# The second mixer's post norm, residual and first feed-forward units, worked in two token sets

## The reference, cut to what matters

```python
def rms_norm(x, g):
    xf = x.astype(jnp.float32)
    y = xf * lax.rsqrt(jnp.mean(xf * xf, axis=-1, keepdims=True) + EPS)
    return (y * g.astype(jnp.float32)).astype(x.dtype)

mix = jnp.matmul(y, w_out)                        # 1024 x 1024: "wo2"
x = x + rms_norm(mix, norm_mix_post)              # "post"
hn = rms_norm(x, norm_ffn_pre)                    # "ffn2"
g = dwconv3(jnp.matmul(hn, w_gate), conv_w, conv_b)
u = jnp.matmul(hn, w_up)                          # 1024 x 2816 each
ff = jnp.matmul(jax.nn.gelu(g, approximate=True) * u, w_down)
x = x + rms_norm(ff, norm_ffn_post)
```

## Time and profile before

| | |
|---|---|
| time, median of 3 runs | 1293.77 us (1291.98 to 1294.85) |
| the profiled execution's own time | 1292.15 us |
| its span in the trace | 1290.3 us |
| PE, PEld busy | 1273.3 us (99%), 1041.1 us (81%) |
| DVE, ACT, POOL busy | 690.6, 394.1, 756.7 us |
| HBM read | 114.71 MB, 91 GB/s over the span |
| granted TensorE clock, mean | 0.997 of full speed |

### The profile page before, as it was taken

How to read it: one execution, slowest core, us unless ns; L and a number is a source line. 1 busy time by engine, 2 the same in 40 slices (tenths; PEclk the granted TensorE clock), 3 DMA queues, 4 the chain that set the end, 5 groups by cost and what they waited for, 6 DMA issues and landing times.

```text
span 1290.3 us, 16120 instructions
## 1 busy us (share of the span) xinstructions
PE 1273.3 (99%) x6432; PEld 1041.1 (81%) x6432; DVE 690.6 (54%) x924; ACT 394.1 (31%) x717; POOL 756.7 (59%) x448
## 2 busy tenths in 40 slices
PE   8999999999999999999999999999899999999998
PEld 6888877888888888888887878778788888888886
DVE  5453563867544432123467878685687744447003
ACT  4332474322111111003246365573322211110002
POOL 5854533676666646768665445224659766666660
PEclk9999999999999999999999999999899999999999
DMA  7222211323333323333233122102133333333231
GB/s 287 82 68 81 82 50 50 111 88 95 98 98 99 99 72 114 90 100 122 96 110 94 55 82 81 35 18 82 50 131 98 98 96 93 95 96 96 97 98 66
DMA packets 34207, 117.85 MB, mean 91 GB/s; under 512 B 3812, under 2 KB 4324, under 8 KB 34004
## 3 DMA queue, kind: packets, MB, share of 16 engines
q1 hardware_dynamic: 32976, 114.66, 28.3%
q10 hardware_dynamic: 1156, 2.16, 0.5%
HBM read 114.71 MB, written 2.10 MB: 91 GB/s over the span
## 4 chain that ended last, share of the span: by engine, by line
PE 97%; DVE 1%; DMA 1%; ACT 1%; issue 0%; POOL 0%; SPq 0%; DVEq 0%; ACTq 0%
PE PS L466 29%; PE PS L468 28%; PE PS L467 28%; PE PS L1083 2%; PE PS L968 1%; PE PS L692 1%; PE PS L669 1%; PE PS L500 1%; PE PS L559 1%; PE PS L501 1%; PE PS L680 1%; PE PS L503 1%; PE PS L951 1%; DMA RAW<-in_w 1%; PE PS L1064 0%; PE PS L942 0%
## 5 line engine op out<-in xcount | busy, mean ns | idle before, releaser
L423 POOL TENSOR_TENSOR WL<-RAW,WH 128x1024 fp32r<-128x1024 f32 (+1 forms) x216 | 509.9, 2361 | 18.0
L420 POOL TENSOR_SCALAR WH<-RAW 128x1024 fp32r<-128x1024 f32 (+1 forms) x216 | 234.2, 1084 | 442.8 <-DMA RAW<-in_w 399.8
L466 PE MATMUL PS<-AH,WH 128*128 128x512 f32 x896 | 351.3, 392 | 2.8 <-DVE AL L1759 1.5
L468 PE MATMUL PS<-AH,WL 128*128 128x512 f32 x896 | 348.8, 389 | 0.0
L467 PE MATMUL PS<-AL,WH 128*128 128x512 f32 x896 | 348.7, 389 | 0.0
L466 PEld LDWEIGHTS PS<-AH,WH 128*128 128x128 f32 x896 | 168.2, 188 | 41.6 <-POOL WL L423 2.4
L468 PEld LDWEIGHTS PS<-AH,WL 128*128 128x128 f32 x896 | 168.2, 188 | 35.2
L467 PEld LDWEIGHTS PS<-AL,WH 128*128 128x128 f32 x896 | 168.3, 188 | 34.5 <-issue 0.2
L1409 ACT ACTIVATE TMP<-PAD,PRM 128x512 f32<-128x512 f32 x44 | 35.9, 816 | 122.5 <-DVE PAD L2022 122.5
L466 PE MATMUL PS<-SH,WH 128*128 128x512 f32 x176 | 68.5, 389 | 0.0
L467 PE MATMUL PS<-SL,WH 128*128 128x512 f32 x176 | 68.5, 389 | 0.0
(11 more groups left out here) (365 smaller groups left out, 2036.0 us busy)
## 6 DMA issues: line engine op xcount, KB each, us to landing
RAW<-in_w SPq DMA_DIRECT2D x185, 512.0 KB, 3.5
RAW<-in_w SPq DMA_DIRECT2D x16, 384.0 KB, 3.1
RAW<-in_w SPq DMA_DIRECT2D x16, 320.0 KB, 2.8
X<-in_x SPq DMA_DIRECT2D x4, 512.0 KB, 7.4
BT<-in_bias SPq DMA_DIRECT2D x1, 2048.0 KB, 9.5
out<-FX SPq DMA_DIRECT2D x4, 256.0 KB, 2.1
out<-FX ACTq DMA_DIRECT2D x4, 256.0 KB, 2.0
PIN<-in_p ACTq DMA_DIRECT2D x1, 512.0 KB, 3.4
```

Of the source, the lines that this page charges most:

```text
L420: nc.gpsimd.tensor_scalar(WH[:, slot, 0:width], RAW[:, slot, 0:width], 1.0, 1.0, ALU.mult, ALU.mult).then_inc(s_hi, 1)
L423: nc.gpsimd.tensor_tensor(WL[:, slot, 0:width], RAW[:, slot, 0:width], WH[:, slot, 0:width].bitcast(F32), ALU.subtract).then_inc(s_split, 1)
L466: nc.tensor.matmul(o, lh, rh, start=start, stop=False)
L468: return nc.tensor.matmul(o, ll, rh, start=False, stop=stop)
```

## The change

The last two projection units and the first four feed-forward units are computed in two token sets, tokens 0 to 255 and 256 to 511 (`HALVES`), each as 256-column matmuls, and so are all steps between them.

- Projection: units 4 and 5 stay whole and go to banks 4 and 5 (no wait any more for a bank to be copied). Units 6 and 7 run for the first set into banks 2 and 3, then for the second set into banks 4 and 5, which wait for `s_mix`.
- Post norm: `post_sum` on VectorE adds the two last squares of a set, `post_columns` takes two columns from `ACC` alone, `post_reciprocal` and `post_diagonal` make one diagonal each on VectorE and ScalarE, `post_broadcast` spreads them into bank 7 (first set) or bank 6 (second). On TensorE those of the first set stand inside the projection's second set, those of the second set inside the feed-forward's first set, at k = 4 and k = 6.
- Residual and pre norm: VectorE takes the 8 tiles of the first set (`post_added`, `post_low`), then their 8 squares in a row (`post_squared`), then the same for the second set. `statistic` waits for all 16 and stands ahead of the last k of the second set.
- POOL splits weights up to the fourth feed-forward unit, then waits until all 16 low parts are made, and splits the fifth and sixth after that. Before it had no wait there.

```diff
-            split_range(UNITS["wo2"][0] + 4, UNITS["ffn2"][0] + NS)
-            split_range(UNITS["ffn2"][0] + NS, NU)
+            split_range(UNITS["wo2"][0] + 4, UNITS["ffn2"][0] + 4)
+            ge(pool, s_gl["ffn2"], 2 * DK)
+            split_range(UNITS["ffn2"][0] + 4, NU)
...
-            def side_by_side(u0, banks, hi, lo, each, before):
-                for n in range(len(banks)):
+            def post_halves(u0, hi, lo, high, low, between):
+                for n in range(4):
...
-                        for n, b in enumerate(banks):
+                for half, c in enumerate(HALVES):
+                    for k in range(DK):
+                        if (half, k) in between:
+                            between[half, k]()
+                        ge(pe, high, DK * half + k + 1)
+                        for n in range(4):
                             s = (u0 + n) % NS
-                            if part == 0:
-                                nc.tensor.matmul(pb[b], WH[:, s, tokens(k)], hi[:, k, :], start=(k == 0), stop=False)
-                                nc.tensor.matmul(pb[b], WL[:, s, tokens(k)], hi[:, k, :], start=False, stop=False)
-                            else:
-                                ins = nc.tensor.matmul(pb[b], WH[:, s, tokens(k)], lo[:, k, :], start=False,
-                                                       stop=(k == DK - 1))
-                                if k == DK - 1:
-                                    ins.then_inc(s_used, 1)
+                            nc.tensor.matmul(pb[n][:, c], WH[:, s, tokens(k)], hi[:, k, c], start=(k == 0), stop=False)
+                            nc.tensor.matmul(pb[n][:, c], WL[:, s, tokens(k)], hi[:, k, c], start=False, stop=False)
+                        ge(pe, low, DK * half + k + 1)
+                        for n in range(4):
+                            s = (u0 + n) % NS
+                            ins = nc.tensor.matmul(pb[n][:, c], WH[:, s, tokens(k)], lo[:, k, c], start=False,
+                                                   stop=(k == DK - 1))
+                            if half and k == DK - 1:
+                                ins.then_inc(s_used, 1)
...
-                ge(pe, s_acc[n], DK)
+                ge(pe, s_acc[n], 2 * DK if n == "ffn2" else DK)
...
-            def root_columns(n):
-                ge(pe, s_acc[n], DK - 1)
-                for part, src in enumerate((ACC, SQ[:, 1, :])):
-                    if part:
-                        ge(pe, s_sq[n], DK)
-                    for t in range(NT):
-                        ins = nc.tensor.matmul(pb[6][:, t:t + 1], src[:, tokens(t)], INVD[:, 0:1],
...
+            def post_columns(half):
+                ge(pe, s_pacc, WHOLE + 2 + 2 * half)
+                for t in range(2 * half, 2 * half + 2):
+                    ins = nc.tensor.matmul(pb[6][:, t:t + 1], ACC[:, tokens(t)], INVD[:, 0:1], start=True, stop=True)
+                ins.then_inc(s_pcol.sem, 1)
...
+            def post_broadcast(half):
+                for t in range(2 * half, 2 * half + 2):
+                    if t % 2 == 0:
+                        ge(pe, s_pdiag, half + 1)
...
+                        ge(pe, s_padiag, half + 1)
+                    ins = nc.tensor.matmul(pb[SPREAD[half]][:, tokens(t)], INVD, DIAG[:, t, :], start=True, stop=True)
+                ins.then_inc(s_pbc.sem, 1)
...
-                    side_by_side(u0, range(4), AH, AL, (s_gh[norm], s_gl[norm]), {DK - 1: lambda: statistic(norm)})
+                    post_halves(u0, AH, AL, s_gh[norm], s_gl[norm],
+                                {(0, 4): lambda: post_columns(1), (0, 6): lambda: post_broadcast(1),
+                                 (1, DK - 1): lambda: statistic(norm)})
...
-            for m in range(WB, DK):
+            for m in range(WB, WHOLE):
                 ready(u0 + m)
-                pe.wait_ge(s_mix, m - WB + 1)
-                col_unit(u0 + m, pb[m % WB], YH, YL).then_inc(s_used, 1)
-            root_columns("post")
-            root_broadcast("post")
+                col_unit(u0 + m, pb[m], YH, YL).then_inc(s_used, 1)
+            for half, c in enumerate(HALVES):
+                for m in range(WHOLE, DK):
+                    s, bank = (u0 + m) % NS, half * 2 + m - WHOLE + 2
+                    ready(u0 + m)
+                    pe.wait_ge(s_mix, bank + 1)
+                    for k in range(DK):
+                        if half and m == WHOLE and k == 5:
+                            post_columns(0)
+                        if half and m == WHOLE + 1 and k == 2:
+                            post_broadcast(0)
+                        ins = mm3(pb[bank][:, c], WH[:, s, tokens(k)], WL[:, s, tokens(k)], YH[:, k, c], YL[:, k, c],
+                                  k == 0, k == DK - 1)
+                    ins.then_inc(s_used if half else s_phalf.sem, 1)
...
+            for m in range(WHOLE):
+                act.wait_ge(s_used, UNITS["wo2"][0] + m + 1)
+                if m >= 2:
+                    ge(act, s_pacc, m - 1)
+                A(SQ[:, m % 2, :], pb[m], ACT.Square).then_inc(s_psq.sem, 1)
+                A(MIX[:, m, :], pb[m], ACT.Copy, scale=prm("post2", m)).then_inc(s_mix, 1)
+            def post_tile(half, m):
+                c, bank = HALVES[half], half * 2 + m - WHOLE + 2
+                if half:
+                    act.wait_ge(s_used, UNITS["wo2"][0] + m + 1)
+                else:
+                    ge(act, s_phalf, m - WHOLE + 1)
+                ge(act, s_pacc, m - 1)
+                A(SQ[:, m % 2, c], pb[bank][:, c], ACT.Square).then_inc(s_psq.sem, 1)
+                A(MIX[:, m, c], pb[bank][:, c], ACT.Copy, scale=prm("post2", m)).then_inc(s_mix, 1)
+            def post_root(half):
+                ge(act, s_pcol, half + 1)
+                A(RCOL[:, 2 * half:2 * half + 2], pb[6][:, 2 * half:2 * half + 2], ACT.Sqrt, bias=prm("eps", 3),
+                  scale=2.0 ** -20).then_inc(s_psd.sem, 1)
+            def post_diagonal(half):
+                t = 2 * half + 1
+                ge(act, s_prc, half + 1)
+                A(DIAG[:, t, :], IDENT, ACT.Copy, scale=RCOL[:, t:t + 1]).then_inc(s_padiag.sem, 1)
+            def post_high(half, m):
+                c = HALVES[half]
+                ge(act, s_x["ffn2"], DK * half + m + 1)
+                A(AH[:, m, c], X[:, m, c], ACT.Copy, scale=prm("fpre2", m)).then_inc(s_gh["ffn2"].sem, 1)
+            def post_square(half, m):
+                if m >= 2:
+                    ge(act, s_acc["ffn2"], DK * half + m - 1)
+                A(SQ[:, m % 2, HALVES[half]], X[:, m, HALVES[half]], ACT.Square).then_inc(s_sq["ffn2"].sem, 1)
+            for m in range(WHOLE, DK):
+                post_tile(0, m)
+            post_root(0)
+            post_diagonal(0)
+            for m in range(3):
+                post_high(0, m)
+            post_tile(1, WHOLE)
+            post_high(0, 3)
...
+            post_high(0, 4)
+            post_tile(1, WHOLE + 1)
+            post_high(0, 5)
+            post_root(1)
+            post_high(0, 6)
+            post_diagonal(1)
+            post_high(0, 7)
             for m in range(DK):
-                act.wait_ge(s_used, UNITS["wo2"][0] + m + 1)
-                norm_tile("post", None, m // 2, 2, m % 2, None, x=pb[m % WB], split=False)
-                A(MIX[:, m, :], pb[m % WB], ACT.Copy, scale=prm("post2", m)).then_inc(s_mix, 1)
-            root_of_columns("post")
-            x_tiles("ffn2", "fpre2", AH)
+                post_square(0, m)
+            for m in range(DK):
+                post_high(1, m)
+            for m in range(DK):
+                post_square(1, m)
             ffn("ffn2", "ffn2", ACT.Gelu_apprx_tanh)
             A(COL[:, 247:248], EPS_C, ACT.Sqrt)
...
             low_turned(range(1, H2))
-            for m in range(DK - 1):
-                add_square("post", m // 2, 2, m % 2)
-            column_reciprocal("post")
-            ge(dve, s_bcast["post"], 1)
+            ge(dve, s_psq, 1)
+            V_.tensor_copy(ACC[:], SQ[:, 0, :]).then_inc(s_pacc.sem, 1)
+            for m in range(1, WHOLE):
+                ge(dve, s_psq, m + 1)
+                ge(dve, s_pacc, m)
+                V_.tensor_tensor(ACC[:], ACC[:], SQ[:, m % 2, :], ALU.add).then_inc(s_pacc.sem, 1)
+            def post_sum(half):
+                c = HALVES[half]
+                for i in range(2):
+                    n = WHOLE + 2 * half + i
+                    ge(dve, s_psq, n + 1)
+                    ge(dve, s_pacc, n)
+                    V_.tensor_tensor(ACC[:, c], ACC[:, c], SQ[:, i, c], ALU.add).then_inc(s_pacc.sem, 1)
+            def post_reciprocal(half):
+                t = 2 * half
+                ge(dve, s_psd, half + 1)
+                V_.reciprocal(RCOL[:, t:t + 2], RCOL[:, t:t + 2]).then_inc(s_prc.sem, 1)
+                ge(dve, s_prc, half + 1)
+                V_.tensor_scalar(DIAG[:, t, :], IDENT, RCOL[:, t:t + 1], None, ALU.mult).then_inc(s_pdiag.sem, 1)
```

(89 more changed lines are left out.)

16 lines of the change are left out of this document (7 added, 9 removed).

## The result

The changed kernel takes 1300.11 us (median of 6 runs, 1299.91 to 1301.48) against 1293.81 (6 runs, 1291.98 to 1294.85): ratio 1.0054, 95% interval 1.0043 to 1.0065. It is slower by 6.3 us.

The account below looks back on a forecast made before the run. It took TensorE as the bound (97% of the chain). Early starts, the second set's held sum and half clock put feed-forward unit 5 at 955.55 instead of 947.47: +8.1, so 1300.2, or 1301.9 against the median; range 1293.5 to 1305.

Parts of the forecast that it names:

- the second set's squares beside POOL: Before the statistic: POOL's four instructions alternate with VectorE's last adds, so the sum is complete at 950.8, not 945.2.
- The steps, as distances from 904.16: On TensorE: feed-forward's first matmul at 918.85, second set 933.4, statistic after a wait to 950.95, unit 5 at 955.55.
- the half tile at 1.19: VectorE's residual and pre norm: a 256-column tile without its square takes 1.19 us.
- the first add held to the end of L423's successor: First set's first add to X waits for POOL's instruction ending at 917.83 and ends at 918.15.
- the copy and adds at 9.1: Second set's squares on VectorE: 7.7 us beside POOL plus 1.4 us for three free adds, together 9.1 us.
- the same 2.35: Behind TensorE's late idle before the statistic: half clock costs 2.35 us, as behind the 7.44 us gap of the kernel before.
- +8.1: Net delay of the feed-forward's unit 5, 955.55 against 947.47, carried to the total time; chance 0.54.
- The idle ahead of the statistic: TensorE idle from 943.1 to 950.95, about 8 us, waiting for the second set's sum of squares.
- TensorE at 0.115 a half matmul: A 256-column matmul takes 0.115 us from start to start, bounds 0.113 and 0.12.
- The idles of 0.8 and 1.75 us: TensorE waits 0.8 us for the first set's broadcast and 1.75 us between projection and the feed-forward's first matmul.
- The rival of no change: POOL doesn't get between the second set's adds: sum at 945.2, +0.0, 1293.8 us; chance 0.14.
- The faster rival: VectorE never held by POOL, half tiles cheaper than 1.19: up to -6.0 us, 1287.8 at half price; chance 0.08.

Follow-up runs that it names:

- run 1: The changed kernel with POOL released only after the 16th square is added, not after the 16th low part: 1295.37 us, ratio 1.0016 to the kernel before.
- run 3: The changed kernel with POOL released by the eighth low part instead of the sixteenth: 1298.19 us, ratio 1.0049 to the kernel before.
- run 4: The changed kernel with the second set's squares added tile by tile in the loop, not in a row afterwards: 1293.07 us, ratio 0.9999 to the kernel before.
- run 7: The changed kernel with both sets' squares in their loops and separate semaphores for the pre norm's counters: 1293.00 us, ratio 1.0000 to the kernel before.
- run 8: run 7 plus the product of MIX and the broadcast placed in PSUM: 1291.55 us, ratio 0.9988 to the kernel before.
- run 5: The changed kernel with TensorE taking the statistic behind the feed-forward's fifth unit: 1296.19 us, ratio 1.0020 to the kernel before.
- run 6: run 5 plus POOL held to two units until the 16 squares are summed: 1293.61 us, ratio 1.0003 to the kernel before.

## Why the prediction was right

- **Direction and place.** Slower was forecast, by the second set's squares beside POOL; runs 1, 3 and 4 show that this is the cause, for the time goes when the overlap goes, and moves when it moves.
- **The steps, as distances from 904.16.** First feed-forward matmul 14.7 forecast, 14.2 measured; second set 29.2 and 29.0; statistic 46.8 and 46.6; fifth unit 51.4 and 50.5. Up to the statistic all of them stood within 0.6 us, and so did what they were made of: the half tile at 1.19, the first add held to the end of L423's successor, the copy and adds at 9.1 (measured 9.3, from 943.53 to 952.81).
- **The term that was mis-sized** is "the same 2.35" for the late clock. The stretch behind the statistic ran at 0.59: (1 - 0.59)/0.5 x 3.91 = 3.2 us at half clock, a loss of 1.6. More of the half-clock time lay in the idle itself and cost nothing (clock 0.69 over 947.10 to 952.87, which is 3.6 us). That is 0.7 of the 0.9 us between +8.1 and the +7.2 of the traces; the other 0.2 came ahead of the statistic.
- **The idle ahead of the statistic** was forecast at 8 us and came to 5.8: TensorE needed 11.8 us for the second set's first seven tiles (935.25 to 947.08) instead of 9.7, with half clock and a pitch of 0.12. The sum set the end, so this moved nothing.
- **TensorE at 0.115 a half matmul** was too low, 0.12 is measured; as said, it did not set the end here. In the second sets of runs 7 and 8 it does, for TensorE has no idle there up to the fifth unit.
- **The idles of 0.8 and 1.75 us** in the projection: the first did not occur, the second was 1.45, and the clock stayed at 1.00 in the first two stretches, as forecast. Behind the one of 1.8 us between the sets it fell (0.84 from 933 to 944 us), which the forecast did not have; it cost nothing, since TensorE waited for the sum anyway. Whether it falls there differs between executions: run 1 has the same idle, and its clock stayed up.
- **The rival of no change** asked that POOL stay out of the adds; run 1 and run 4 make it so, and land at 1295.4 and 1293.1. Its 1293.8 was right for run 4. The price of the split that run 1 puts on TensorE's path was left out of it.
- **The faster rival** asked for cheap half tiles and for a VectorE that POOL never holds. Half tiles are not cheap, and with the sums free of POOL (run 4, where the first add to X is still held) the two sets only reach the kernel before. Two prices stand against the 4.2 us won at the start: VectorE's narrow instructions (two half tiles with squares 3.05 us where a whole one took 2.59, 3.7 over eight) and TensorE's 1.9. They lie on two engines side by side, and no run separates them.
- **Not settled:** the medians differ by 6.3 us, the distances in the two traces by 7.2. The runs of before spread over 2.9 us, and the trace after is of the slowest of its six runs (1301.48), so one trace of each doesn't decide between them. That the clock's part comes to 1.6 us in other executions too was not measured apart.

The Trainium skill (SBUF — State Buffer, "Who interferes with whom") says that a VectorE instruction with at most one SBUF input outside the 2-port modes does not contend with GpSimd. Run 8 agrees: 0.42 us for the add with a PSUM operand beside POOL's instruction, 2.42 with two SBUF operands. A single SBUF tensor is not enough by itself, though: the diagonal, a copy with a scale, took 1.14 us beside POOL and 0.29 alone.

## What to carry to other kernels

Before a stage is cut into two halves, price the engine whose chain leads to its end: here a half tile on VectorE cost 60% of a whole one, and that is 3.7 us against an earlier start of 4.2. When an engine is released by the last of a row of steps, look at what stands behind that step in the same list; an instruction order that keeps two-SBUF-operand work of VectorE out of POOL's run, or moves one operand to PSUM, can be worth more than the overlap (run 4 took 7.0 us off, the earlier start is 4.2). And after shortening a wait, ask whom the earlier release feeds: in run 5 it was POOL, which took back 4.3 of the 7.4 us that run 6 gains in D7 (by the medians 2.6 of 6.5).

## What the runs showed of the hardware

- VectorE and POOL took strict turns: in the rows of adds one of VectorE's passed between two of POOL's, even where POOL's next was due 0.08 us later (seven adds 3.60, 8.88 and 12.21 us beside none, four and more POOL instructions).
- Three 256-column matmuls took 0.36 us, 0.12 each with a weight load each, against 0.227 at 512 columns: half the columns cost 53%.
- The granted clock could fall behind an idle of 1.8 us between stretches of half-width matmuls, and could as well stay up. The changed kernel and runs 1, 4, 5 and 6 run the same instructions up to the second set and idle 1.77 to 1.79 us ahead of it: the clock went to its lower level (1.2 GHz) in the traces of the changed kernel (0.50 from 937 to 939 us) and of runs 4 and 6, and stayed at 1.00 in those of runs 1 and 5. So one trace does not tell what such an idle costs. In run 8, whose idles were 0.75, 1.3 and 1.0 us, it stayed at 1.00.
